# A two-layer diffusion backbone on one core: the token mixer's units and stages in a new order

## What is computed

```
u = hin @ w_in                       # hq hi hg hf | mq mk mv mo mi mf | mz xbc dt | bg
y_hg = head_rms(hgrn2(silu(hq), kk, hi, logf), g) * silu(hg)          # both directions
y_ml = head_rms(mlstm(mq, mk, mv, mi, mf), g) * sigmoid(mo)           # both directions
xbc  = silu(dwconv3(xbc)); mx, B, C = split(xbc)                      # centred, 3 taps, 768 channels
y_mb = rms((ssd(mx, dt, B, C) + d * mx) * silu(mz), g)                # both directions
y    = sum_c sigmoid(bg[c]) * (y_c @ w_branch[c]) @ w_out             # c = hg, ml, mb
```

## Time and profile before

| | us |
|---|---|
| median of 3 runs | 2873.17 (2867.31 to 2878.22) |
| the profiled execution | 2881.43, span 2879.6 |
| TensorE busy | 2483.8 (86%) |
| GpSimd busy | 1478.8 (51%) |
| VectorE busy | 1231.0 (43%) |
| ScalarE busy | 1080.1 (38%) |
| mean granted clock of TensorE | 0.916 |

### The profile page before, as it was taken

The page is one execution under the profiler, slowest core; times in us unless marked ns, Lnnn a source line. Parts: engine busy times, 40 slices in busy tenths (PEclk is TensorE's granted clock), DMA queues, the critical chain, the costliest instruction groups (busy, mean ns, idle before and its releaser), DMA issues.

```text
span 2879.6 us, 37405 instructions
## 1 busy us (share of the span) xinstructions
PE 2483.8 (86%) x13354; PEld 2237.3 (78%) x13354; DVE 1231.0 (43%) x1710; ACT 1080.1 (38%) x1687; POOL 1478.8 (51%) x644
## 2 busy tenths in 40 slices
PE   5599989998878868899949999999877887789995
PEld 2399989886656648899949998988766565789995
DVE  3454227561256246554135421756224723635412
ACT  4432235324343442532333223532343444253322
POOL 3365554554547654455525555445444765436551
PEclk7799999999789979999979999999888898889998
DMA  6433333233334423233323333323332443223331
GB/s 239 147 132 125 118 107 125 88 117 125 121 116 144 161 95 103 96 125 128 114 67 118 129 113 122 112 94 117 120 124 95 162 143 125 88 88 132 124 114 62
DMA packets 100339, 343.71 MB, mean 119 GB/s; under 512 B 11632, under 2 KB 17008, under 8 KB 99824
## 3 DMA queue, kind: packets, MB, share of 16 engines
q1 hardware_dynamic: 92880, 333.00, 34.1%
q10 hardware_dynamic: 7328, 8.97, 0.9%
HBM read 337.73 MB, written 4.20 MB: 119 GB/s over the span
## 4 chain that ended last, share of the span: by engine, by line
issue 46%; POOL 34%; PE 15%; DVE 2%; DMA 1%; POOLq 1%; ACT 1%; ACTq 0%; DVEq 0%; SPq 0%; PEldq 0%
POOL wlo L489 34%; PE ps L522 4%; PE ps L524 4%; PE ps L523 4%; DMA raw<-in_w_mod 1%; PE ps L531 1%; POOLq L499 1%; PE ps L877 1%; PE ps L878 1%; PE ps L879 0%; PE ps L901 0%; POOLq L429 0%; PE ps L551 0%; PE ps L553 0%; PE ps L552 0%
## 5 line engine op out<-in xcount | busy, mean ns | idle before, releaser
L489 POOL TENSOR_TENSOR wlo<-raw,whi 128x1024 fp32r<-128x1024 f32 (+2 forms) x640 | 1478.6, 2325 | 1352.4 <-ACT whi L943 1277.4
L943 ACT CAST whi<-raw 128x1024 fp32r<-128x1024 f32 (+1 forms) x640 | 654.3, 1038 | 861.4 <-DMA raw<-in_w_gu 403.3
L522 PE MATMUL ps<-h_hi,whi 128*128 128x384 f32 x2176 | 756.0, 347 | 49.5 <-ACT modr L1114 19.2
L523 PE MATMUL ps<-h_lo,whi 128*128 128x384 f32 x2176 | 746.4, 343 | 0.0
L524 PE MATMUL ps<-h_hi,wlo 128*128 128x384 f32 x2176 | 745.3, 343 | 0.0
L522 PEld LDWEIGHTS ps<-h_hi,whi 128*128 128x128 f32 x2176 | 424.4, 195 | 71.7 <-POOL wlo L489 35.3
L523 PEld LDWEIGHTS ps<-h_lo,whi 128*128 128x128 f32 x2176 | 423.6, 195 | 1.3 <-issue 0.8
L524 PEld LDWEIGHTS ps<-h_hi,wlo 128*128 128x128 f32 x2176 | 423.1, 194 | 0.0
L522 PE MATMUL ps<-act_hi,whi 128*128 128x384 f32 x704 | 239.6, 340 | 9.4 <-DVEq L439 9.4
L531 PE MATMUL ps<-whi,cond_s 128*4 128x512 f32 x368 | 174.9, 475 | 80.3 <-POOL wlo L489 52.2
L524 PE MATMUL ps<-act_hi,wlo 128*128 128x384 f32 x704 | 239.3, 340 | 0.0
(11 more groups left out here) (287 smaller groups left out, 3147.9 us busy)
## 6 DMA issues: line engine op xcount, KB each, us to landing
raw<-in_w_in SPq DMA_DIRECT2D x288, 512.0 KB, 3.5
raw<-in_w_gu SPq DMA_DIRECT2D x176, 512.0 KB, 3.4
raw<-in_w_down SPq DMA_DIRECT2D x64, 512.0 KB, 3.4
raw<-in_w_mod SPq DMA_DIRECT2D x40, 512.0 KB, 4.4
raw<-in_w_down SPq DMA_DIRECT2D x32, 384.0 KB, 2.9
raw<-in_w_branch SPq DMA_DIRECT2D x24, 512.0 KB, 3.4
raw<-in_w_out SPq DMA_DIRECT2D x16, 512.0 KB, 3.4
x<-in_x ACTq DMA_DIRECT2D x1, 1536.0 KB, 6.6
```

What stands on the lines that cost most here:

```text
L489: nc.gpsimd.tensor_tensor(wlo[s][:, 0:w], raw[s][:, 0:w], whi[s][:, 0:w].bitcast(F32), ALU.subtract).then_inc(w_split, 1)
L522: mm(out, hi_, xh[:, xc, :], start=start and n == 0, stop=False)
L523: mm(out, hi_, xl[:, xc, :], start=False, stop=False)
L943: act.copy(whi[s][:, 0:w], raw[s][:, 0:w]).then_inc(w_hi, 1)
```

## The change

The planner now plans single units. `weave` lays a modulation item's four units between the parts of a projection; item by item a bank is assigned and `clear_of` says whose evacuation frees it. What lies where:

| phase | units, in order (m: modulation unit, t: turn) |
|---|---|
| hd | gr gr hf hf, m m hf m m hf hf t, twice; hq x4, hi, hg |
| hg | m m mv, m mv, m mv, mv, t m m mo, m mo, m mo, mo, t m m, m m mq, mq, t m m mq, m m, mq mk, t mk, mk, mk, nothing |
| n0 (norm of HGRN) | m m m m xbc t m m m; m xbc; t |
| ml (rows only) | xbc xbc; xbc; xbc; bg; bg bg; bg; bg; bg |
| nm | m m mz m mz m mz; mz; t |
| si | m m m m bg; bg t, three times |
| sp | m m m m; bg; bg; t m m; m m bg; nothing; bg; t m m m; m bg; bg; t; m m bg; m; m bg; bg; t |
| n2 (norm of SSD) | m m m m bg t m m m m bg; bg; t |

The phase "cv" and three meetings are gone. The convolution reads its taps from the PSUM bank of the block, in the norm of HGRN (blocks 0, 1) and in mLSTM rows 1 to 3 (blocks 2 to 5); a later unit in that bank waits for the closing step. The SSD states alternate the two directions with a tile each, and one product of two factors is made once for all tiles. The transposes into tokens use two pairs of banks. ScalarE copies the first two branch inputs within the norm of SSD, VectorE makes their low parts there and behind it, and `adaln` moves from behind the SSD rows to the fourth block of the branches. The evacuations of mz and of n0, nm, n2 are no longer held back.

```diff
-    "ml": between(named("xbc", 6) + named("bg", 6), (3, 4, 5, 6, 7)),
-    "nm": [("mz", 0)],
-    "cv": runs((6, 7, 8, 9), (8, 9)),
-    "si": runs((10, 11, 12, 13, 14, 15), (10, 11)),
-    "sp": runs(range(16, 24), range(12, 18)),
+    "n0": weave(parts_of("xbc", 0, 2), (6, 7)),
+    "ml": parts_of("xbc", 2, 6) + parts_of("bg", 0, 6),
+    "nm": weave(parts_of("mz", 0, 1), (8,)),
+    "si": weave(parts_of("bg", 6, 12), (9, 10, 11)),
+    "sp": weave(parts_of("bg", 12, 21), (12, 13, 14, 15)),
+    "n2": weave(parts_of("bg", 21, 24), (16, 17)),
...
+            def conv_out(b, bank):
+
+                act.wait_ge(sd_w, b + 1)
+                af(bank[:, 0:T], cbuf[b % 2][:, :], ACT.Tanh).then_inc(cv_t, 1)
...
+            def taps(l, b):
+
+                bank, c = ps[made["xbc", b][3][0]], cbuf[b % 2]
+                tap = lambda j: convh[:, 3 * b + j:3 * b + j + 1]
+                if b >= 2:
+                    dve.wait_ge(post, POST_CV + b - 1)
+                unit_done(dve, l, UM + made["xbc", b][2][0])
+                step(ts(c[:, :], bank[:, 0:T], tap(1), convh[:, 18 + b:19 + b], ALU.mult, ALU.add))
+                step.done()
+                for first, end in GROUPS:
+                    step(stt(c[:, first + 1:end], bank[:, first:end - 1], tap(0), c[:, first + 1:end], ALU.mult,
+                             ALU.add))
+                step.done()
+                for first, end in GROUPS:
+                    last = stt(c[:, first:end - 1], bank[:, first + 1:end], tap(2), c[:, first:end - 1], ALU.mult,
+                               ALU.add)
+                last.then_inc(sd_w, 1)
+
+            def conv_done(b):
+
+                dve.wait_ge(sd_w, b + 1)
+                dve.wait_ge(cv_t, b + 1)
+                stt(xs[:, b, :], ps[made["xbc", b][3][0]][:, 0:T], 1.0, cbuf[b % 2][:, :], ALU.add,
+                    ALU.mult).then_inc(post, 1)
...
                 for t in range(NT):
+                    if b == 0:
+                        convolved(l, "n0", t)
...
                 for r in range(8):
                     if r < 6:
                         exps(r + 2, r % 2)
+                    if r:
+                        for b in XBC["ml", r - 1]:
+                            taps(l, b)
                     scores(r, ps[3], r // 2 + 1)
                     weights(r)
+                    if r:
+                        for b in XBC["ml", r - 1]:
+                            conv_done(b)
                     if r:
                         heads(r - 1)
                     carry(r)
...
                 for t in range(NT):
+                    if b == 2:
+                        act.wait_ge(sd_y, t + 1)
                     af(flat[:, t * MIX:(t + 1) * MIX], src(t), ACT.Square).then_inc(nm_sq, 1)
-                if keys:
+                if b == 0:
                     keys_out()
-                    act.wait_ge(stored, phase[0] * (16 * STORES) + 64)
+                    act.wait_ge(stored, l * (16 * STORES) + 64)
+                if b == 2:
+                    branch_in(0, y_hg)
+                    branch_in(1, y_ml)
                 act.wait_ge(nm_ms, b + 1)
...
+                state(0, 0, 1, 0)
+                pe.wait_ge(st_loaded, 48)
+                inter(0, 1, 0)
+                inter(1, 2, 0)
+                state(1, 0, 2, 1)
+                fill(l, "si", 3)
+                state(0, 1, 3, 4)
+                fill(l, "si", 4)
+                state(1, 2, 4, 5)
+                inter(0, 2, 5)
+                fill(l, "si", 5)
+                inter(1, 1, 6)
+                pe.wait_ge(sd_o, 8)
...
-                normed(l, 2)
-                meet(pe, MEET["br_in", 0])
+                clear("sp", 3, 7)
+                normed(l, 2, "n2")
                 branches(l)
```

602 lines of the change are left out of this document (310 added, 292 removed).

## The result

The changed kernel takes 2831.1 us in the median of four runs (2828.9 to 2834.4), beside 2875.7 us for the kernel before: a ratio of 0.984, 95% interval 0.982 to 0.986. It is 44.6 us faster. The forecast was 2795 us, a gain of 80; the time lies in the forecast's range and next to the first rival (2835). Measured once more, later, it took 2825.3 us (2821.3 to 2830.6), ratio 0.982 (0.980 to 0.983). So differences under some 6 us between two kernels of this study are not read from the time alone; there the traces decide.

The account below looks back on a forecast made before the run. TensorE was taken to bound the kernel, its losses lying in places. The stage terms summed to -40 us a mixer, -80 for both: 2801 us, 2793 on the median's scale, stated as 2795, range 2745 to 2850.

Parts of the forecast that it names:

- What bounds the kernel: Whole kernel: TensorE has the work, busy 86% of the span, and loses in places, some 170 us a mixer.
- Head: Mixer's head: 8 modulation units and 2 turns add 9.8 us, plus split and turn waits; +17, bounds +11 and +22.
- mLSTM: mLSTM stage: only feature-major units in slots, rows near 6.7 us; 113.6 to 86 us, -28, bounds -36 and -8.
- SSD rows: SSD rows: work 81 us, two turn waits, nearly empty rows; 102.6 to 89 us, -13.6, bounds -20 and -6.
- Branches: Branches: VectorE's modulation sums move to the fourth block and hide behind 12.5 us of products; 0, bounds -2 and +4.
- First norm: First norm with meeting: 3.5 us less work, new 4.4 us wait, two split losses go; -2, bounds -7 and +5.
- SSD states: SSD states: 47.2 us of work against 43, stage 54.7 to 55 us; 0, bounds -3 and +8.
- Third norm: Third norm: fifth unit's split waits for ScalarE, 17 us after opening; 25.3 to 43 us, +17.7, bounds +9 and +25.
- Output: Layer norm behind the mixer: fourth block's tanh changes the table, so its root pays another 1.28 us; +1.3.
- Rival 1: Split-weight supply falls dry elsewhere: mLSTM rows 9 us (+18), SSD rows gain only lighter work (+3); 2835 us, chance 0.20.
- rival 2: Covers hold better: head -5, mLSTM loses 10 in place of 24 (-9), third norm -5; 2755 us, chance 0.15.
- rival 3: Slower: VectorE bounds the dense stages as two-SBUF-operand products wait for splits; +17 a mixer, 2907 us, chance 0.06.

Follow-up runs that it names:

- turns apart: Changed kernel with, in SSD states and rows, a feature-major unit moved so no modulation unit follows a turn in the same bank: 2812.9 us, ratio 0.977.
- matmuls behind the turns: Changed kernel plus six unused 384-column matmuls into a free bank behind five turns of the SSD states and rows, order kept: 2825.2 us, ratio 0.981.
- one block a row in mLSTM: Changed kernel with a gate unit and one convolution block in mLSTM's first slot, then one block a row: 2809.6 us, ratio 0.975.

## Why the prediction was right or wrong

**What bounds the kernel**: right. TensorE's work stayed, and the mixer's gain of 23.8 us is some 19 us of idle time and 2 of low clock. mLSTM and the convolution's stage together came to -69.7 us where -67.8 was forecast; some 30 us of that are idle time and low clock (50.4 us before, 20.7 after), the rest is work that now stands in other stages. The three parts that were to give some of it back (head +16.6, levels +4.4, third norm +18.2) are within 1 us of +17, +5 and +17.7.

**Head**: right, with its mechanism: waits for splits of 1.5 and 2.6 us in the first units, low clock of 1.7. Only the cause in the order, "now they are modulation units", is less than it seemed: with two feature-major units first the waits stand elsewhere and come to the same 4.1 us.

**mLSTM**: right. No wait for a split is left in it; one for the closing step in row 1 took 6.3 us:

```profile
PE ps L562 <- DVE xs L1552: 6.3, 1, 6.3
```

From one product with the carried state (line 805) to the next, rows 5 and 6 take 6.4 us each (forecast 6.7), row 4, which holds two units and a wait of 1.2 us, 12.8. A convolution block costs 0.67 + 2 x 0.47 + 2 x 0.35 + 0.55 = 2.9 us of VectorE, not 2.4, as a first tap from PSUM takes 0.67. The bounds' upper end, 6.0 us, was wrong for the reason taken from the earlier trace rows. The rule of the Trainium skill that the prediction names beside it (SBUF — State Buffer, Who interferes with whom), that one SBUF operand outside the two-port modes doesn't contend and two do, stands: the traces agree in each of the three places where they could break it: the taps from PSUM, the taps from SBUF with two such operands (up to 2.31 us), and the product of the third norm (0.69 against 2.7 us).

**SSD rows**: the step that failed most, by 10.5 us. The work (81) came as 81.0 and the idle time (7.6) as 7.5; the second is partly luck, since the waits for turned rows took 4.2 us where 2.3 was forecast and the rest 3.3 where it was 5.3. The sum had no term for low clock, since before the stage ran at 0.97 with waits of the same 1.14 us. After, it ran at 0.88: 11.0 us. A row of before showed what happened to the clock then; it was read as a property of the pattern, and it was not one. Behind the entry the falls stand at waits of 1.2 to 1.8 us. Three edits took them away in part or in whole: turns apart, matmuls behind the turns, and one block a row in mLSTM, which left this stage's order as it was. So the waits are where the clock falls, and not by themselves why. Some 5 of the 11.0 us stand at the entry (907.5 to 917.7 us), behind waits of 1.7 and 0.6 us for the last state and the first decay; this is the part that the matmuls behind the turns left.

**Branches**: "hide behind its 12.5 us of products" failed, by 6.0 us. The products were there, but the sums stood ahead of the one product that frees TensorE's bank. Seven small instructions, six of 0.2 us and one that took 2.2 beside a split, held the product back by 3.6 us; with it TensorE waited 4.8 us, and the clock fell. VectorE's total was reckoned where its order counts; moved to the block's last product, the sums leave waits of at most 1.3 us in that stage.

**First norm**: the wait of 4.4 us came as 4.6, but "two of the losses for splits go" failed: 3.1 us of waits for splits stayed of 3.5, and a turn's bank added 1.2 (2.0 in place of 0.8). Idle rose by 5.7 us. The miss is 3.9 us.

**SSD states** 2.6 us over, inside the bounds: the share of it was not taken apart.

**Third norm**: right in size (43.4 us, forecast 43) and in the first cause, ScalarE's stream. The hit has some luck in it. The forecast has the squares done 11.1 us behind the opening of the stage (1062.3 less 1051.2) and the root at about 1065, though the copies (2.9) and the table load (1.28) end at 1066.5 by its own figures; the squares were done after 8.6 us, and the fifth unit was used 16.5 us behind the opening, for 17 forecast. GpSimd sat idle 16.3 us, TensorE waited 13.6:

```profile
1017.75 1.28 ACT L1155 ACT_TABLE_LOAD   x1
...
1019.25 3.87 ACT L993 CAST whi<-raw 128x1024 fp32r<-128x1024 f32 x4
...
1020.35 4.87 POOL L529 TENSOR_TENSOR wlo<-raw,whi 128x1024 fp32r<-128x1024 f32 x2 [16.33 <-ACT whi L993]
```

But ScalarE's order was only the first of three limits. Behind it stood VectorE's stretched product with the modulation row's copy, and behind these waits for splits of 6.0 us, which are GpSimd's pace in part. With the first two mended, 5.6 us came of the 13 that the first alone had promised.

**Output**: the table load of 1.28 us in the layer norm behind the mixer is there:

```profile
1157.39 1.28 ACT L1050 ACT_TABLE_LOAD   x1
```

**The sum.** Of the forecast -40 a mixer the misses take 10.5 (SSD rows), 6.0 (branches), 3.9 (first norm) and 2.6 (states), and 7.0 go the other way (output 2.4, mLSTM 1.9, second norm 1.5, the rest 1.2): -24.0, measured -23.8. The time is in the range because the range was wide; of the gain that was forecast, 56% came. **Rival 1** has the number but not the cause: it put +18 into mLSTM rows of 9 us, which took 6.4, and waits for splits play no part in the SSD rows (0.3 us). Its number is also off by its own prices: SSD rows that gain only their lighter work (86.7 us before, 81 after) gain 5.7 us and not 13.6, which is +8 and not +3, so it should have read some 2845. In rival 2, mLSTM with 10 us lost in place of 24 would be -14, not -9 (2745, not 2755). And three large bounds to the fast side give 2729, not 2740. Of **rival 3** the mechanism is real, but it decides where a split runs beside a product with two SBUF operands, and in the HGRN levels that did not become more frequent:

```profile
L1636 DVE TENSOR_TENSOR kk<-kk,fd x14: 944/954/3157, 564.2 to 667.3; 128x768 f32<-128x768 f32 x14
```

The median is that of the earlier trace rows. For the other product of a level (qa, 14 times) it went from 1.27 to 1.33 us.

**What stays open.** What decides whether a wait of 1.2 us costs low clock as well: the profiles give 11.0 us in the SSD rows for both mixers of the changed kernel, twice measured, and 4.3 us where mLSTM was 7 us shorter. No run shows which difference between the two matters, and so none says how much of what turns apart and matmuls behind the turns gained in these rows is due to the waits and how much to such a difference. The end of the branches, where TensorE waits 4.8 us for the last remainder, and the entry of the SSD rows were not tried.

## What to carry to other kernels

Price a stage in three terms, work, idle time and low clock, and give the third a range of its own wherever a wait of a microsecond is left: it was the part that moved without being touched. When work is hidden behind an engine's other work, look at which of its instructions frees the buffer that somebody waits for, and put the hidden work behind that one. When a stall has one clear cause in an in-order stream, read what stands next in line before its whole length is counted as gain.

## What the runs showed of the hardware

- With six useless matmuls behind each of three turns the SSD rows were 4.5 and 5.2 us shorter: added work can pay through the granted clock (0.88 before, 0.95 and 0.96 with it). In the SSD states, with two turns treated so, it cost 1.1 and 2.7 us. The one-block kernel reached 94.7 us without such matmuls, so that filling the waits is not shown to be the only way by which they work.
- Where the clock falls is repeatable: the changed kernel shows a loss of 11 us in the SSD rows in both mixers of both of its profiles, at the same instructions, and the same waits in the one-block kernel lose 4.3. Waits for splits of 1.2 and 1.3 us, in the run with turns apart, cost no low clock at all in these rows.
- A tensor_scalar of 384 columns takes 0.67 us from PSUM and 0.47 from SBUF, but beside a split the one from SBUF took 2.69 and the one from PSUM never over 0.68. It has one SBUF operand of full size; the Trainium skill (SBUF — State Buffer, Who interferes with whom) states that such instructions can enter a two-port mode and then contend, and this trace agrees.
